# Attention scores as two row tiles of float32r parts and values as two column tiles in a hybrid encoder layer

## What is computed

```python
def attend_block(q_blk):
    sc = jnp.einsum("bqkgd,bskd->bkgqs", q_blk, k).astype(jnp.float32)
    pr = jax.nn.softmax(sc, axis=-1).astype(v.dtype)
    return jnp.einsum("bkgqs,bskd->bqkgd", pr, v)
```

## Time and profile before

| what | value |
|---|---|
| median of 3 runs | 1226.73 us (1225.0 to 1227.09) |
| profiled execution: span from first to last instruction | 1227.0 us |
| PE busy | 1125.2 us (92%) |
| DVE busy | 850.3 us (69%) |
| ACT busy | 602.9 us (49%) |
| POOL busy | 364.2 us (30%) |
| attention and SSD stage | about 237 to 401 us |

### The profile page before, as it was taken

One profiled execution on the slowest core, in us unless ns is written; L12 is line 12 of the kernel. 1 busy time (PEld: TensorE's weight loads), 2 busy tenths in 40 slices (PEclk: granted clock), 3 DMA queues, 4 the chain that ended last, 5 costly groups with the idle time before them and its releaser, 6 DMA issues.

```text
span 1227.0 us, 13573 instructions
## 1 busy us (share of the span) xinstructions
PE 1125.2 (92%) x4706; PEld 736.3 (60%) x4706; DVE 850.3 (69%) x1026; ACT 602.9 (49%) x741; POOL 364.2 (30%) x275
## 2 busy tenths in 40 slices
PE   5999869789998999999999999999999999999950
PEld 3568758565665454344466777777777777777630
DVE  5436783557778154273358888988888889988738
ACT  1143244456575110110256676687666776787522
POOL 0007992244544000000100333322333333322313
PEclk9999889979999999999999999999999999999985
DMA  9010100300000930200559999999999999999815
GB/s 331 6 69 4 66 1 1 103 1 1 1 1 2 317 136 35 94 26 26 175 214 332 384 382 389 390 379 390 384 395 381 385 389 395 382 386 380 311 29 202
DMA packets 74886, 253.86 MB, mean 207 GB/s; under 512 B 7384, under 2 KB 9304, under 8 KB 74848
## 3 DMA queue, kind: packets, MB, share of 16 engines
q1 hardware_dynamic: 69440, 234.49, 50.1%
q0 software_dynamic: 5408, 18.88, 5.7%
HBM read 237.62 MB, written 15.73 MB: 206 GB/s over the span
## 4 chain that ended last, share of the span: by engine, by line
PE 80%; DVE 9%; POOL 5%; issue 2%; ACT 2%; DMA 1%; SPq 0%; ACTq 0%; DVEq 0%; POOLq 0%
PE ps L1880 15%; PE ps L1882 14%; PE ps L1881 14%; PE ps L1792 7%; PE ps L1760 7%; PE ps L1558 4%; PE ps L1664 2%; PE ps L1679 2%; PE ps L1552 2%; PE ps L1861 2%; PE ps L1797 2%; DVE xT L1451 1%; DVE ring L1206 1%; PE ps L1790 1%; PE ps L1655 1%
## 5 line engine op out<-in xcount | busy, mean ns | idle before, releaser
L1327 DVE TENSOR_TENSOR low<-late,high 128x2048 fp32r<-128x2048 f32 x192 | 427.1, 2283 | 31.5 <-ACT high L698 31.5
L698 ACT ACTIVATE high<-late 128x2048 fp32r<-128x2048 f32 x192 | 354.9, 1914 | 24.0 <-DMA late<-in_w_e_up 23.7
L661 POOL COPY idx_now<-idxT 96x1 int32 (+1 forms) x30 | 132.7, 4423 | 375.3 <-DVE xa L1368 203.2
L1880 PE MATMUL ps<-high,xeT 128*96 128x512 f32 x528 | 210.8, 399 | 6.8 <-issue 4.8
L1882 PE MATMUL ps<-high,xeT 128*96 128x512 f32 x528 | 208.9, 396 | 0.0
L1881 PE MATMUL ps<-low,xeT 128*96 128x512 f32 x528 | 208.4, 395 | 0.0
L1880 PEld LDWEIGHTS ps<-high,xeT 128*96 128x96 f32 x528 | 86.0, 163 | 43.3 <-issue 6.1
L1882 PEld LDWEIGHTS ps<-high,xeT 128*96 128x96 f32 x528 | 85.9, 163 | 37.7 <-issue 0.5
L1881 PEld LDWEIGHTS ps<-low,xeT 128*96 128x96 f32 x528 | 86.0, 163 | 36.3 <-issue 0.3
L1880 PE MATMUL ps<-high,hidT 128*96 128x512 f32 x240 | 95.5, 398 | 2.3 <-DVE low L1327 2.3
L1882 PE MATMUL ps<-high,hidT 128*96 128x512 f32 x240 | 94.2, 393 | 0.0
(11 more groups left out here) (255 smaller groups left out, 1858.1 us busy)
## 6 DMA issues: line engine op xcount, KB each, us to landing
late<-in_w_e_gate SPq DMA_DIRECT2D x64, 1024.0 KB, 6.9
late<-in_w_e_up SPq DMA_DIRECT2D x64, 1024.0 KB, 8.0
late<-in_w_e_down SPq DMA_DIRECT2D x64, 1024.0 KB, 8.1
ring<-in_w_in SPq DMA_DIRECT2D x3, 2048.0 KB, 9.1
ring<-in_w_ple_gate SPq DMA_DIRECT2D x2, 2048.0 KB, 11.5
ring<-in_w_in SPq DMA_DIRECT2D x3, 1024.0 KB, 13.0
x_rows<-xa POOLq DMA_DIRECT2D x6, 512.0 KB, 2.9
acc_rows<-mix POOLq DMA_DIRECT2D x12, 256.0 KB, 2.3
```

What stands on the lines that cost most here:

```text
L661: return nc.gpsimd.tensor_copy(idx_now[:, col:col + 1], idxT[:, bass.ds(e, 1)])
L698: return nc.scalar.activation(o, i, ACT.Copy)
L1327: nc.vector.tensor_tensor(low[j], raw[j], high[j], ALU.subtract).then_inc(s_low, 1)
L1880: nc.tensor.matmul(o, lhs[0][:, k, :], high[j][:, c], start=(k == 0), stop=False)
```

## The change

Scores: the queries and keys are no longer copied once as float32. ACT writes their float32r high parts (`qh`, `kh`), and DVE subtracts these from PSUM and writes the float32r rests (`ql`, `kl`) in a new step `qk_low(t)`, put among the state updates for tiles 0 to 3 and behind them for tiles 4 and 5. The zero-padded keys and POOL's memset are gone. The two units of a pair (same head index j, both key/value groups) are now neighbours, and `scores` issues them together at even steps: three float32r products each (high x high, high x low, low x high), one unit on partitions 0 to 63 and the other on 64 to 127, alternating, into two PSUM banks. The pair waits for the exponential of the unit two before its first.

Values: one `pv` per token tile instead of one per group. For each key tile it has two float32 products of 64 value columns, one per group, that write output partitions 0 to 63 and 64 to 127 of one bank. It waits for all eight units of the tile and stands at step 8t+11, ahead of that step's `turn` and `before`. `att_out` copies all 128 rows once per tile. `pt_out` for tile t waits for the values of tile t-1.

SP: the layer norm's rows are loaded after the last score, since `ql` of tiles 3 to 5 lies in their place.

The diff, without the declarations of semaphores and most of the context:

```diff
         gA, bA = gb_in[:, 0, :], gb_in[:, 1, :]
-        qT = xT[:, 0:4, :]
-        kz = xT[:, 4:6, :]
         s0, s1 = ring[:, 0, :], ring[:, 1, :]
...
         xrows = late[:, KC * PADW:KC * PADW + 4 * CW]
+
+        qh = over("qh", "xT", 0, [P, NT, 512])
+        kh = over("kh", "xT", 4 * T, [P, T])
+        kl = over("kl", "xT", 5 * T, [P, T])
+        ql_part = [over("ql0", "xT", 6 * T, [P, 3, 512]), over("ql1", "gB", 0, [P, 3, 512])]
+
+        def ql(t):
+            return ql_part[t // 3][:, t % 3, :]
         tri_r = over("tri_r", "late", NT * 768, [P, 2, P])
...
         U_XB, U_QK = NT + 1, 2 * NT + 1
-        att_units = [(t, 4 * i + j) for t in range(NT) for i in range(NKV) for j in range(4)]
+        att_units = [(t, i, j) for t in range(NT) for j in range(4) for i in range(NKV)]
         NU = len(att_units)
...
             load_wout(2, 0)
+            sp.wait_ge(s_sc, NU)
             sp.dma_start(gB[:], bc(A["ln1_g"][0])).then_inc(s_ln1, 16)
             sp.dma_start(bB[:], bc(A["ln1_b"][0])).then_inc(s_ln1, 16)
-            sp.wait_ge(s_ao, NG)
+            sp.wait_ge(s_ao, NT)
             sp.wait_ge(s_yo, NG)
...
             for n in range(0, len(upd), 2):
-                if n == len(upd) // 2 + 2:
-                    pool.wait_ge(s_proj, len(groups))
-                    nc.gpsimd.memset(kz, 0.0).then_inc(s_kz, 1)
                 if n:
...
                 n += 1
-            act.wait_ge(s_kz, 1)
             for t in range(NT):
                 u = U_QK + t
                 act.wait_ge(s_tr, u + 1)
                 b = 2 * (u % 2)
-                tc = slice(t * P, (t + 1) * P)
-                copy(qT[:, :, tc], ps[:, b, :].rearrange("p (j c) -> p j c", j=4))
-                for i in range(NKV):
-                    last = copy(kz[i * HD:(i + 1) * HD, i, tc], ps[i * HD:(i + 1) * HD, b + 1, 0:P])
-                last.then_inc(s_qkT, 1)
+                copy(qh[:, t, :], ps[:, b, :])
+                copy(kh[:, t * P:(t + 1) * P], ps[:, b + 1, 0:P]).then_inc(s_qkh, 1)
             def probabilities(u):
...
             nc.vector.tensor_tensor(dtw[:, WDEC, :], dtw[:, WDEC, :], dtw[:, DT, :], ALU.mult).then_inc(s_cums, 1)
+            def qk_low(t):
+                dve.wait_ge(s_qkh, t + 1)
+                b = 2 * ((U_QK + t) % 2)
+                tc = slice(t * P, (t + 1) * P)
+                nc.vector.tensor_tensor(ql(t), ps[:, b, :], qh[:, t, :], ALU.subtract)
+                nc.vector.tensor_tensor(kl[:, tc], ps[:, b + 1, 0:P], kh[:, tc], ALU.subtract).then_inc(s_qkT, 1)
+
             dve.wait_ge(s_cums, 2)
...
                     nc.vector.tensor_tensor(new, new, prod, ALU.add).then_inc(s_sts, 1)
+                if n > len(upd) // 2 and n % 2:
+                    qk_low((n - len(upd) // 2) // 2)
+            for t in range(len(upd) // 4, NT):
+                qk_low(t)
             def row_max(u):
...
             def pt_out(u):
-                n = seq_of[att_units[u][0]][1]
+                t, i, j = att_units[u]
+                n = seq_of[t][1]
                 dve.wait_ge(s_pt, u + 1)
-                if u >= 8:
-                    dve.wait_ge(s_pv, u // 4 - 1)
-                nc.vector.tensor_copy(probT[u // 4 % 2][:, 0:n, (u % 4) * P:(u % 4 + 1) * P],
+                if t:
+                    dve.wait_ge(s_pv, t)
+                nc.vector.tensor_copy(probT[i][:, 0:n, j * P:(j + 1) * P],
                                       ps[:, 3, 0:n * P].rearrange("p (b c) -> p b c", c=P)).then_inc(s_pts, 1)
-            def att_out(G):
-                t, i = G // NKV, G % NKV
-                dve.wait_ge(s_pv, G + 1)
-                nc.vector.tensor_copy(mix[i * HD:(i + 1) * HD, t, 0:512],
-                                      ps[i * HD:(i + 1) * HD, 4, :]).then_inc(s_ao, 1)
+            def att_out(t):
+                dve.wait_ge(s_pv, t + 1)
+                nc.vector.tensor_copy(mix[:, t, 0:512], ps[:, 4, :]).then_inc(s_ao, 1)
             def weights(n):
...
                     pt_out(i - 3)
-                if i % 4 == 0 and i >= 8:
-                    att_out(i // 4 - 2)
+                if i % 8 == 4 and i >= 12:
+                    att_out(i // 8 - 1)
                 if i % 4 == 0 and 4 <= i <= NU:
...
-            def scores(u):
-                t, h = att_units[u]
+            def scores(u0):
+                t, _, j = att_units[u0]
                 a, n = seq_of[t]
-                if u >= 3:
-                    pe.wait_ge(s_exp, u - 2)
-                nc.tensor.matmul(ps[:, u % 3, 0:n * P], qT[:, h % 4, t * P:(t + 1) * P],
-                                 kz[:, h // 4, a * P:(a + n) * P], start=True, stop=True).then_inc(s_sc, 1)
+                if u0 >= 2:
+                    pe.wait_ge(s_exp, u0 - 1)
+                jc = slice(j * P, (j + 1) * P)
+                for step, (q, k) in enumerate(((qh[:, t, jc], kh), (qh[:, t, jc], kl), (ql(t)[:, jc], kh))):
+                    for i in range(NKV):
+                        rows = slice(i * HD, (i + 1) * HD)
+                        last = nc.tensor.matmul(ps[:, (u0 + i) % 3, 0:n * P], q[rows], k[rows, a * P:(a + n) * P],
+                                                start=(step == 0), stop=(step == 2))
+                        if step == 2:
+                            last.then_inc(s_sc, 1)
             def turn(u):
...
                 last.then_inc(s_pt, 1)
-            def pv(G):
-                a, n = seq_of[G // NKV]
-                pe.wait_ge(s_pts, 4 * G + 4)
-                if G:
-                    pe.wait_ge(s_ao, G)
+            def pv(t):
+                a, n = seq_of[t]
+                pe.wait_ge(s_pts, 8 * t + 8)
+                if t:
+                    pe.wait_ge(s_ao, t)
                 for b in range(n):
-                    last = nc.tensor.matmul(ps[:, 4, :], kvd[:, a + b, P:2 * P], probT[G % 2][:, b, :],
-                                            start=(b == 0), stop=(b == n - 1))
+                    for i in range(NKV):
+                        last = nc.tensor.matmul(ps[i * HD:(i + 1) * HD, 4, :],
+                                                kvd[:, a + b, P + i * HD:P + (i + 1) * HD], probT[i][:, b, :],
+                                                start=(b == 0), stop=(b == n - 1))
                 last.then_inc(s_pv, 1)
...
             for i in range(NU + 4):
-                if i < NU:
+                if i < NU and i % 2 == 0:
                     scores(i)
+                if i >= 11 and i % 8 == 3:
+                    pv((i - 11) // 8)
                 if i % 4 == 0:
...
                     before(i // 4)
-                if i >= 7 and i % 4 == 3:
-                    pv((i - 7) // 4)
             def out_proj(t, h):
...
             mix_turn(3)
-            pe.wait_ge(s_ao, NG)
+            pe.wait_ge(s_ao, NT)
             pe.wait_ge(s_yo, NG)
```

More of the change, by code:

```diff
@@ L242, in hymba_layer @@
         s_rope = sem("s_rope")
-        s_kz = sem("s_kz")
+        s_qkh = sem("s_qkh")
         s_tap = sem("s_tap")
```

## The result

The change made the kernel slower: **1249.44 us** (median of five runs, 1242.33 to 1250.34) against 1226.26 us of before (five runs, 1225.0 to 1227.09), a ratio on record of **1.0171 [1.0157, 1.0185]** (the two medians alone divide to 1.0189). The forecast was 1224.0 us with a range up to 1239. The profile shown here is of the shortest of the five runs, 1242.33 us with a span of 1240.4.

The account below looks back on a forecast made before the run. TensorE held the attention stage's long gaps, DVE close behind; a loop over engines held the short ones. 1227.0 + 3.2 - 0.7 - 6.7 + 1.0 = 1223.8, rounded to 1224.0 us; range 1218 to 1239.

Parts of the forecast that it names:

- Clock: Attention stage: longer pause at the start and lighter short gaps invite one more half-clock stretch; +1.0 us (0 to +3).
- The clock falls in the long gaps: Rival: PE loses work from 296 us on, half of the value gaps run at half clock; +9, 1233 us, chance 0.10.
- Scores 0.7 us a pair, values 3.43 us a tile: TensorE's score and value products: row tiles and column tiles run side by side, down from 1.72 and 6.86 us.
- column tiles one after the other: Rival: a tile's values stay 6.86 us, in one piece ahead of `before`; +15.4, 1239.5 us, chance 0.22.
- row tiles one after the other: Rival: score pairs do not overlap, +0.7 in three value gaps and some 0.7 in short ones; about 1227 us, chance 0.10.
- The sign that the prediction named for the first of them: Values of 6.9 us, and DVE's idle time before L1217 growing by over 3 us per tile.
- Switching of tile shapes: TensorE running empty at shape changes: 0 to about 0.17 us each, three per value gap; taken as 0, 1.5 in the range.
- The start: Before the first scores: DVE's subtracts for low parts add work, first scores at 240.5 instead of 237.33; +3.2 us (+1 to +5).
- scores starting before 239: Sign that the prediction is wrong: first scores were expected at about 240.5 us.
- Short gaps: Five gaps between `decay` starts, 237.65 to 295.73 us: `att_out` once per tile instead of twice; -0.7 us (0 to -1.4).
- Long gaps: Six gaps between `decay` starts, 295.73 to 378.32 us: 12.2 without values, 13.1 with, 75.9 against 82.59; -6.7 (-3 to -9).
- The layer-norm loads: SP's two loads move behind the last score but still land before first use; 0 us.

Follow-up runs that it names:

- the first filler: Changed kernel plus float32 products nobody reads where TensorE waits: at the start, ahead of `y`, around `turn`; 1223.28 us, 0.9971 of before.
- the better one: Changed kernel, filler placed anew: five products ahead of the first `y`, two ahead of the first state product, none just ahead of the values; 1219.63 us, 0.9938.
- with the clock held in both: Changed kernel with the better-placed filler, 1219.63 us, against the kernel before with filler at the start and in its short gaps, 1224.33 us.

## Why the prediction was wrong

The step that failed is **"Clock", +1.0 (0 to +3)**, with its rival "The clock falls in the long gaps" at +9 and a chance of 0.10. The direction of that rival was right; its size and its chance were not. By the runs, the clock cost the changed kernel 26 us (against the first filler) to 30 us (against the better one), and the kernel before 3 us. Without the clock term the sum of the prediction is +3.2 - 0.7 - 6.7 = -4.2 us; measured with the clock held in both, -4.7. That these agree so well is in part luck: the terms below came out at +1.9, -1.4 and -5.7, and the misses nearly cancel.

Three steps in that argument were wrong. *"It stayed at 1.00 from 296 on"* was a row of a kernel whose PE was 93% busy; the gap without values was just what the change would empty. Its own share could have been worked out from the prediction's terms: `decay` 1.98, four `turn`s 1.84, `before` 0.87, two pairs of scores 1.4 and `y` 0.8, some 6.9 of 12.2 us (`cb` left out; the trace of after has PE busy for 7.9 to 8.3 us of these gaps), and the earlier trace rows had a fall behind a window at 1.96 of four. *"a half clock fills PE again"* is true, and the windows of after show it at 324 to 328; but the full clock is then lost again in the next gap, so the price comes once for each gap with values, not once. And it was priced at *half* of a value gap's PE work; the three gaps lost 15.99 + 18.88 + 18.45 less 40.40 of the same three with the better filler, 12.9 us, and the short gaps, for which the prediction had only the +1.0 of one more stretch, some 8 to 12 more (65.39 against 57.11 and 53.71). The four runs that were not profiled took 6 to 8 us longer still; their mean granted clock over the whole execution is lower too, 0.932 to 0.934 against 0.938, but no trace shows where.

Point by point:

- *Scores 0.7 us a pair, values 3.43 us a tile:* the tiles run side by side, as forecast; values were right, and a pair of scores takes 0.90 us to the product behind it, 0.2 more. The rivals "column tiles one after the other" (0.22) and "row tiles one after the other" (0.10) fell with the first timeline. The sign that the prediction named for the first of them was no good test: at half clock the values of a tile took up to 5.8 us (351.75 to 357.53) and DVE stood 8.9 us ahead of the offset terms from 296 to 379, where before it had not waited there. Only the starts of two tiles within 0.01 us tell the two causes apart.
- *Switching of tile shapes, 0 to 0.5 us a gap, taken as 0:* inside its bounds, and perhaps not 0. With the better filler the first pair of a tile's values starts at 310.44 and the product behind them at 314.02, 3.58 us, where eight full-width products took 3.43; with the 0.2 of the scores that is at most some 0.35 us in a gap with values; no run separates the switch from other causes of these tenths. The Trainium skill (TensorEngine Tiling (Array Packing), Key Properties) says that a change of tiling mode drains TensorE; this trace leaves no room for more than that 0.35 us.
- *The start, +3.2 (+1 to +5):* a loss, as forecast, and smaller. From the first state product of the second half to the first scores it took 13.95 us instead of 12.05, +1.9. The subtracts cost what was costed, DVE's records:

```profile
224.58 0.69 DVE L1155 TENSOR_TENSOR ql<-ps,qh 128x512 fp32r<-128x512 f32 x1
225.18 0.28 DVE L1156 TENSOR_TENSOR kl<-ps,kh 128x128 fp32r<-128x128 f32 x1
```

  That is 0.69 and 0.28 where 0.25 was taken. The first scores came at 235.97, not 240.5, and not only for that: in this execution the stage began 3.3 us earlier than in the profile of before, in code that is the same in both. Counted from the start that before had, they would stand at 239.2, so the sign "scores starting before 239" rests on that shift.
- *Short gaps, -0.7:* after, +7.3, at half clock. With the clock held in both, 53.71 against 55.07: -1.4, the good end of the range. The prediction's reading that a loop, not PE, held these gaps in before was only partly right: with the clock held before took 55.07 for them instead of 58.08, so 3 us were PE at half clock.
- *Long gaps, -6.7 (-3 to -9):* after, +6.8. With the clock held -5.7: gaps without values 12.00, 12.15 and 12.31 (forecast 12.2), gaps with them 13.34, 13.34 and 13.72 (forecast 13.1). The values start 6.5 us into such a gap (310.44 - 303.93; forecast 6.8); in the changed kernel, at half clock, 9.2 (323.06 - 313.91).
- *The layer-norm loads, 0:* right. They are issued at 396.20 and 396.60 and first used at 447.92.
- *What would prove it wrong:* "clock under 0.9 after 296" was on that list, and it is what came.

One thing stays open. With the clock held, `out_proj` starts 6.7 us earlier in the changed kernel (391.28 against 397.96), and the time gains 4.7; the rest of the program took 826.5 us in the one and 824.6 in the other. Before and after without filler took 825.9 and 825.2, so the spread between executions is of that size; it was not followed up.

## What to carry to other kernels

In this kernel, work taken off TensorE in a stage that another loop paces did not only come back as idle time: it took the clock from the products that stay. Before such a change, work out how busy TensorE will be in each part of the loop's period, not in the mean, and look in the trace for parts as light as the lightest one and for the granted clock right behind them. Where it falls, work that nobody reads, put where TensorE waits, can be worth more than the change itself: here the change alone lost 1.7%, and with such filler it gained 0.6%.

## What was not expected of the hardware

- A kernel with more products on TensorE ran faster, twice: the scores done twice (1240.44 against 1249.44 us), and with filler (69 records of it from 296 to 379, 1223.28 us).
- The kernel before, too, got slower when its scores were made lighter (1230.41 us), and faster when it was given work for nothing (1224.33).
- Two column tiles of float32 run fully beside each other: 0.43 us a pair at full clock, which is the time of one full-width record, and 0.85 at half (352.66, 353.51, 354.36).
